# One Trainium2 core, a two-block model: the expert loop's gather in column groups, its scatter one expert later

## What is computed

```python
# 256 tokens, 16 experts, each takes its best 32 tokens
aff = jax.nn.softmax((h @ w_router).astype(jnp.float32), axis=-1)
gate, idx = lax.top_k(jnp.swapaxes(aff, 1, 2), cap)
xg = h[bidx, idx]
a = jnp.einsum('becd,edf->becf', xg, w1)
b = jnp.einsum('becd,edf->becf', xg, w3)
ye = jnp.einsum('becf,efd->becd', jax.nn.silu(a) * b, w2) * gate[..., None].astype(h.dtype)
return jnp.zeros_like(h).at[bidx, idx].add(ye)
```

## Time and profile before

| | us |
|---|---|
| median of 3 runs | 2255.59 |
| lowest and highest | 2252.48, 2257.17 |
| the profiled execution | 2257.46 |
| its span in the trace | 2255.7 |
| busy: PE, DVE, ACT | 1953.8, 760.5, 328.4 |

### The profile page before, as it was taken

One profiled execution on the slowest core, in us unless ns is written; L12 is line 12 of the kernel. 1 busy time (PEld: TensorE's weight loads), 2 busy tenths in 40 slices (PEclk: granted clock), 3 DMA queues, 4 the chain that ended last, 5 costly groups with the idle time before them and its releaser, 6 DMA issues.

```text
span 2255.7 us, 29584 instructions
## 1 busy us (share of the span) xinstructions
PE 1953.8 (87%) x12460; PEld 1354.3 (60%) x12460; DVE 760.5 (34%) x1755; ACT 328.4 (15%) x743; POOL 0.2 (0%) x4
## 2 busy tenths in 40 slices
PE   8999989877677767677666789999999999999999
PEld 5787777332232222232232248868889888688899
DVE  3766463000000000000000035662565536625554
ACT  4131121000000000000000021351110103602100
POOL 0000000000000000000000000000000000000000
PEclk9999999877777787877887789999999999999999
DMA  9276678799999999999999985543635544346441
GB/s 351 90 259 234 233 286 343 302 415 430 429 428 421 428 428 416 428 414 429 429 418 428 428 318 175 188 181 130 244 137 187 207 168 171 147 168 240 153 168 57
DMA packets 148937, 648.85 MB, mean 288 GB/s; under 512 B 10676, under 2 KB 17441, under 8 KB 124198
## 3 DMA queue, kind: packets, MB, share of 16 engines
q1 hardware_dynamic: 145036, 643.78, 72.2%
q10 hardware_dynamic: 3802, 3.65, 0.5%
HBM read 646.36 MB, written 1.05 MB: 287 GB/s over the span
## 4 chain that ended last, share of the span: by engine, by line
PE 64%; DMA 30%; DVE 4%; ACT 1%; issue 1%; SPq 0%; ACTq 0%; DVEq 0%
DMA ring<-in_w_exp 29%; PE bank L2277 15%; PE bank L954 13%; PE bank L2973 6%; PE bank L2006 6%; PE bank L1646 4%; PE bank L2888 3%; PE bank L2027 2%; PE bank L1875 2%; PE bank L971 2%; PE bank L2048 2%; PE bank L701 1%; PE bank L1000 1%; PE bank L1571 1%; PE bank L998 1%
## 5 line engine op out<-in xcount | busy, mean ns | idle before, releaser
L2006 PE MATMUL bank<-ring,arena 128*32 128x512 f32 x1984 | 289.5, 724 | 154.7 <-DMA ring<-in_w_exp 153.7
L954 PE MATMUL bank<-hx,ring 128*128 128x256 f32 x1344 | 293.9, 380 | 0.0
L2006 PEld LDWEIGHTS bank<-ring,arena 128*32 128x32 f32 x1984 | 61.7, 122 | 364.1 <-DMA ring<-in_w_exp 240.2
L954 PEld LDWEIGHTS bank<-hx,ring 128*128 128x128 f32 x1344 | 254.4, 190 | 37.1 <-issue 3.0
L2027 PE MATMUL bank<-ring,arena 128*32 128x512 f32 x992 | 150.9, 748 | 81.3 <-DMA ring<-in_w_exp 70.5
L2091 DVE COPY arena<-bank 128x256 f32<-128x256 f32 x15 | 6.4, 425 | 506.1 <-PE bank L2011 506.1
L2277 PE MATMUL bank<-arena 128*128 128x256 f32 x672 | 150.9, 379 | 0.0
L2027 PEld LDWEIGHTS bank<-ring,arena 128*32 128x32 f32 x992 | 31.4, 129 | 185.3 <-DMA ring<-in_w_exp 106.9
L2277 PEld LDWEIGHTS bank<-arena 128*128 128x128 f32 x672 | 127.1, 190 | 16.9
L1881 DVE TENSOR_TENSOR arena<-bank,arena 128x256 f32<-128x256 f32 x16 | 6.8, 425 | 321.0 <-PE bank L1875 321.0
L2277 PE MATMUL bank<-ring,hx 128*128 128x256 f32 x448 | 105.9, 379 | 0.0
(11 more groups left out here) (535 smaller groups left out, 2323.2 us busy)
## 6 DMA issues: line engine op xcount, KB each, us to landing
ring<-in_w_exp SPq DMA_DIRECT2D x185, 2048.0 KB, 16.1
ring<-in_w_ada SPq DMA_DIRECT2D x36, 2048.0 KB, 13.0
ring<-in_w_in SPq DMA_DIRECT2D x29, 2048.0 KB, 7.9
ring<-in_w_ffn_in SPq DMA_DIRECT2D x20, 2048.0 KB, 8.0
ring<-in_w_ffn_out SPq DMA_DIRECT2D x10, 2048.0 KB, 7.9
ring<-in_w_out SPq DMA_DIRECT2D x6, 2048.0 KB, 10.3
arena<-in_w_exp SPq DMA_DIRECT2D x4, 2048.0 KB, 15.7
ring<-in_w_up_nsa SPq DMA_DIRECT2D x2, 2048.0 KB, 9.2
```

What stands on the lines that cost most here:

```text
L954: ins = pe.matmul(b[:, o:o + n], w[:, k, j * P:(j + 1) * P], h[:, k, :], start=k == 0, stop=k == KD - 1)
L2006: ins = pe.matmul(banks[s][32 * j:32 * j + 32, :], e_xe[:, 2 * t + kk, :], w[:, kk, 512 * j:512 * j + 512], start=t + kk == 0, stop=t + kk ...
```

## The change

Five edits.

- The gather has its operands swapped: `e_ps` (32 columns) is stationary and 256 columns of the tokens move, four matmuls side by side in the column groups, 8 in all. The result has tokens on partitions, so ACT copies it (`e_gx`) and two transposes turn it (`pe_gather_turn`); DVE adds the shift in two halves.
- In `body` the gather stands behind the second of the last four tiles and the turn behind the third. The last expert, which gathers nothing, has a small matmul in each place that only counts the semaphore.
- The scatter moves to the next expert, between its tiles 3 and 4. PE begins the next expert when ACT has copied the first half of y (`y half copied`) and DVE has written `e_xe`.
- The first half of expert 0's tile 8 (1 MiB) is loaded early, into `hx`, once the tokens are transposed; the other half follows at `expert used0`. In `pe_route`, `pe_still` puts 5, 2, 3 and 3 matmuls of zeros around the waits of the first gather.
- `dve_tables` is called after the first half of the filter sums and not after all of them.

```diff
     def pe_gather(pe, name):
-        for t in range(4):
-            for kk in range(2):
-                o = banks[2][:, (2 * t + kk) * CAP:(2 * t + kk + 1) * CAP]
-                for c in range(NC):
-                    ins = pe.matmul(o, e_htok[:, c, 256 * t + kk:256 * (t + 1):2], e_ps[:, c, :], start=c == 0, stop=c == NC - 1)
+        for c in range(NC):
+            for j in range(4):
+                ins = pe.matmul(banks[2][32 * j:32 * j + 32, 0:256], e_ps[:, c, :], e_htok[:, c, 256 * j:256 * j + 256],
+                                    start=c == 0, stop=c == NC - 1)
         ins.then_inc(*PE.step(f"{name}gathered"))
+    def pe_gather_turn(pe, name):
+        for kk in range(2):
+            ins = pe.transpose(banks[2][:, 256 + kk * P:256 + (kk + 1) * P], e_gx[:, kk::2], ident[:, :])
+        ins.then_inc(*PE.step(f"{name}turned"))
...
+    def pe_still(pe, n):
+        for _ in range(n):
+            pe.matmul(banks[7][:, :], e_y[:, 0:P], e_y[:, 0:512], start=True, stop=True, skip_group_check=True)
...
                 pe.wait_ge(*at("xe", back=1))
-                pe.wait_ge(*at("y copied", back=1))
+                pe.wait_ge(*at("y half copied", back=1))
             for s in range(2):
+                if s and first:
+                    pe.matmul(banks[7][:, 0:N], e_y[:, 0:P], e_y[:, 0:N], start=False, stop=True,
+                              skip_group_check=True).then_inc(*PE.step("scattered"))
+                elif s:
+                    pe.wait_ge(*at("y copied", back=1))
+                    pe.wait_ge(*at("G", back=1))
+                    for j in range(KD):
+                        ins = pe.matmul(banks[4 + j // 2][:, (j % 2) * N:(j % 2 + 1) * N], e_y[:, j * P:(j + 1) * P], e_G,
+                                            start=False, stop=True, skip_group_check=True)
+                    ins.then_inc(*PE.step("scattered"))
...
-        for t, old in ((8, 0), (9, 1)):
-            sp.wait_ge(*at(f"expert used{old}"))
-            expert_tile(ring_of[t], 0, t)
+        sp.wait_ge(*at("expert used0"))
+        n = ring_of[HALF]
+        sp.dma_start(place(n, P, 4, D)[:, 2:4, :], w[:, 2:4, :]).then_inc(tile_sem(n), 16)
+        sp.wait_ge(*at("expert used1"))
+        expert_tile(ring_of[9], 0, 9)
```

68 lines of the change are left out of this document (47 added, 21 removed).

## The result

The changed kernel takes 2242.54 us (median of 5 runs, 2239.14 to 2244.68), the kernel before 2253.04 (median of 5, 2252.48 to 2257.17). The ratio is 0.9947, 95% interval 0.9935 to 0.996: faster by 9 to 15 us. The profiled execution took 2240.68 (span 2238.6), where the one of before took 2257.46. Forecast: 2237 in a range of 2232 to 2246. So sign and range held, and the gain is 10.5 us by the medians where 19 were forecast: half a per cent, small but clear of noise.

What follows compares the result with a forecast made beforehand. Weight loads bound the expert loop, PE the rest. Start 4.6, hole behind expert 0 6.3 and loop boundaries 8.1 sum to 19.0 us, so 2237 us against the median; range 2232 to 2246, some 0.85.

Steps and rivals of the forecast that it cites:

- What bounds the kernel: Expert loop bound by weight loads, but the queue runs dry at some boundaries where PE comes late; elsewhere PE bounds.
- the five holes were skew between the engines: Rival on the loop: skew between 16 engines made the holes, so they stay; gain 10.9, time 2245, chance 0.10.
- The loop, 8.1 us: Boundaries between experts: `used0` comes 10 us sooner, so five holes in the load rate close; 8.1 us, bounds 6 to 8.5.
- The margin of the scatter: Scatter now ahead of tile 4: queue stays busy until 39.2, tile 4 used at about 33, some 5 us to spare.
- The start, 4.6 us: First ada tiles: PE starts 2.2 us earlier and the clock stays up, another 2.4; sum 4.6, bounds 0 to 4.7.
- a load in the wait's place at 2241: Rival at the start: a load takes the place of PE's wait; gain 14.4, time 2241, chance 0.08.
- the clock falling at 2239: Rival at the start: the clock falls all the same; gain 16.6, time 2239, chance 0.15.
- Before expert 0: First gather: expert 0 starts 1.7 us later, at 401.5; zeros holding the clock return 2.4 less 0.4; `used0` stays.
- zeros had eaten the gather's gain: Ahead of expert 0: quick gather (0.9 against 7.01 us) by itself brings nearly nothing, since matmuls of zeros take its time.
- The hole behind expert 0, 6.3 us: Load 4 of expert 1 follows without a hole, landing at 441.1 for 447.4; gain 6.3 us, bounds 3.9 to 7.
- Tile 8's early half: Expert 0's tile 8, first half loaded early: saves 2.4 us of queue where it waits for PE anyhow; costed at nothing.
- The base: Start of the sum: profiled execution of 2257.5, 1.9 above the median of three; less 19.0 gives 2238.5, or 2236.6 against that median.

Runs made afterwards that it cites:

- e2: Kernel before with only the table copies (`dve_tables`) moved forward on DVE; median 2255.18 us, ratio to before 1.0005.
- e12: Changed kernel with gather, turn and scatter all behind the last y tile at the expert boundary, gather in its new form; median 2246.51 us, ratio 0.9973.
- e8: Changed kernel with eight more 512-column matmuls ahead of tile 0 of experts 1 to 15; median 2248.83 us, ratio to before 0.9974.
- e4: Changed kernel with seven early filler matmuls of 256 columns replaced by three of 512, 16 instructions fewer; median 2240.01 us, ratio to before 0.9938.
- e11: Changed kernel with one more filler matmul of 256 columns ahead of the first ada tile, four instructions more; 2243.88 us in one run.
- e5: Changed kernel without any of the 13 matmuls of zeros ahead of expert 0; median 2239.37 us, ratio to before 0.9937.
- e6: Changed kernel with expert 0's tile 8 loaded whole at `used0`, no early half; median 2243.92 us, ratio to before 0.9953.
- e9: Changed kernel with seven 256-column fillers put as three of 512, and zeros 1, 1, 1, 0 for 5, 2, 3, 3; median 2233.96 us, ratio 0.9909.
- e7: Changed kernel with the scatter back at the expert boundary, behind the wait for all of y; median 2243.98 us, ratio to before 0.9956.

## Why the prediction came out as it did, step by step

- **What bounds the kernel: right.** The loop stands at 426 to 430 GB/s in every slice of every kernel that has the new gather, wherever it stands. The rival that the five holes were skew between the engines is out.
- **The loop, 8.1 us: 8.1 measured.** The mechanism was right, the exact hit is luck: the same loop took 2.9 us more in e2 than in the trace that rows 3 were read from. That these holes close because PE comes sooner was right, and so was the size: load 4 was issued at most 8.8 us behind tile 11's landing where it had been up to 17.8, 9 us sooner at the slowest boundaries. e12 (12.9) and e8 (14.9) show that a third to a half of the shortening would have done. The margin of the scatter (5 us to spare) was right in sign: with matmuls of 7.6 us ahead of it (e8) the chain still doesn't meet it.
- **The start, 4.6 us: 0.7 measured; this step failed.** Its two parts were both right as far as they went: PE began at 28.35 (28.3 forecast), and 127 records took 3.69 us (3.9 for 128). In its place stood 2.07 us in the middle of a tile, and a granted clock of 0.76 and 0.50 behind it, 1.70 us. e4 took the stall away and the third ada tile came 5.0 us earlier; e11 moved it by exactly the instructions that were added. The range named a load in the wait's place at 2241 and the clock falling at 2239; the time measured lies beside these, but neither mechanism was the one.
- **Before expert 0: right in the mechanism, and what it meant was not drawn.** The zeros held the clock (1.00), expert 0 began 16.6 us behind the clearing (16.4 forecast: 401.5 less 385.09), the gather took 1.07 (0.9), the turn 0.39 (0.3). `used0` at 403.03 on a clock 0.7 us early is the "same place" of the forecast. The sentence that zeros had eaten the gather's gain was true, and stronger than written: ten of the thirteen do nothing but cost, 6.4 us from clearing to load 4, and with none at all (e5) load 4 comes 6.1 us sooner too.
- **The hole behind expert 0, 6.3 us: 3.7 measured; the term was mis-sized.** `used0` of expert 1 was to come at 433.3 (48.2 behind the clearing); its load was issued at 432.96 (48.5). Load 3 landed at 435.2, 50.8 behind the clearing (51.2 by the forecast). Both right. The wrong step is "loads 2 and 3 then keep the queue full to about 435, so load 4 follows without a hole": load 4 landed 7.8 us behind load 3 and not 4.89. It was issued 2.2 us ahead of load 3's landing, the forecast gave a load 1.3 us to begin to move, and still 2.9 us were lost. The row behind the 1.3 was misread, since the load with 7.4 us was issued 2.5 us ahead of the landing of the one before it, at 426.7; but loads into a really empty queue took 7.4 (e8) to 8.1 us (before, e2), so the figure was near. What failed is that such a delay was taken for all that a load issued ahead has to pay: only loads issued 4.7 us ahead or more lost nothing, but for one with 0.3 (table below). The 3.7 itself is of one pair: against e2 the gain at this place would be nothing, and the loop's 11.0.
- **Tile 8's early half, costed at nothing: at most about 1 us** (e6).
- **The base.** The sum was made against the profiled execution, which lay 1.9 us over the median then known and 4.4 over the median of five. Part of it was a dip of the clock at 2032 that belongs to no kernel. Of the 8.5 us that the gain fell short by the medians, 3.9 are the start, 2.6 are load 4, and 2 are within what landmarks and medians differ by. The time came nearer than the gain (2242.5 against 2237) by luck: the median that the forecast started from was 2.6 us above that of five runs.

## To carry to other kernels

In such a loop find how late PE may be before anything is lost, and shorten the work to that; moving it further brought nothing in this loop. And matmuls that only hold the clock belong where PE waits anyhow, one for each wait, and are to be compared with none at all: thirteen cost 6.4 us against three here, and none (e5) was 0.3 us behind three (e9) at load 4.

## What the runs showed that I had not expected

- PE can stand for 1.94 to 2.34 us in the middle of a tile, waiting for nothing that the trace shows (nine kernels). The end of the stall follows the end of a 16384-byte packet on the queue "instruction" by 1.2 to 1.4 us.
- The same stall was followed by a fall of the clock in six kernels (L480's 20 records in 10.45 us) and not in three (8.75 us; e5, e7, e11). Nothing in the programs differed there, so a gain at this place has a spread of 1.7 us of its own.
- A load issued shortly ahead of its predecessor's landing still loses time. Load 4 of each of the 15 experts behind the first, in all 14 traces (ahead: from its issue to load 3's landing; lost: what it landed behind load 3 beyond 4.89 us):

```
issued ahead, us   cases   lost, us
behind the landing   3     4.5 to 7.1
0.5 to 1.4           4     1.3 to 2.6
1.7                  9     0.8 to 1.9
2.2 to 4.3          16     0.0 to 3.0
4.7 and more       178     0.0 (one 0.3)
```

What sets the loss between 2.2 and 4.3 no run tested. Packets of 16384 bytes in the changed kernel, per us:

```
us    packets  mean ns  max ns
426   30       611      613
431   30       611      611
434   27       489      1461   (with small ones)
436   22       686      1665
438   20       727      1027
442   29       572      653    (with small ones)
```

In the full stream each takes 611 ns; from 433 to 441, behind the issue of load 4 at 432.96, single ones take up to 1665. Before, in the first us behind the empty queue, the mean was 1290 ns. Load 4's 10.1 us go with these slow packets; why they are slow stays open.
